# Six slots for the decode rows, six PSUM places for the memory's products, a later input load and one moved product

## What is computed

```python
def mem_kv(mem, g_mem, w_xkv):                       # 256 memory rows, 16 products of 128 features
    kk, vv = jnp.split(rmsnorm(mem, g_mem) @ w_xkv, 2, axis=-1)
    return kk.reshape(B, M, 4, 256), vv.reshape(B, M, 4, 256)

def cross_attn(xn, mk, mv, w_xq, w_xo):
    q = (xn @ w_xq).reshape(B, T, 4, 256)
    s = jnp.einsum('bthd,bmhd->bhtm', q, mk) * 256 ** -0.5
    p = jax.nn.softmax(s, axis=-1)
    return jnp.einsum('bhtm,bmhd->bthd', p, mv).reshape(B, T, 1024) @ w_xo

h = h + hybrid_mixer(rmsnorm(h, g_mix), ...)         # short conv and mLSTM heads
h = h + cross_attn(rmsnorm(h, g_cross), mk, mv, w_xq, w_xo)
h = h + swiglu(rmsnorm(h, g_ffn), w_gu, w_down)
```

## Time and profile before

| | us |
|---|---|
| median of 3 runs | 2920.24 (2918.0 to 2922.61) |
| the profiled execution | 2920.7 |
| its span, first to last instruction | 2918.9 |
| PE busy | 2865.0 (98%) |
| DVE busy | 1179.5 (40%) |
| ACT busy | 753.7 (26%) |
| POOL busy | 428.6 (15%) |
| mean granted TensorE clock | 0.993 |

### The profile page before, as it was taken

One profiled execution on the slowest core, in us unless ns is written; L12 is line 12 of the kernel. 1 busy time (PEld: TensorE's weight loads), 2 busy tenths in 40 slices (PEclk: granted clock), 3 DMA queues, 4 the chain that ended last, 5 costly groups with the idle time before them and its releaser, 6 DMA issues.

```text
span 2918.9 us, 38362 instructions
## 1 busy us (share of the span) xinstructions
PE 2865.0 (98%) x15739; PEld 2699.9 (92%) x15739; DVE 1179.5 (40%) x2258; ACT 753.7 (26%) x1467; POOL 428.6 (15%) x284
## 2 busy tenths in 40 slices
PE   7899999999999999999999999999999999999998
PEld 7788878888899999999998999998999999999998
DVE  6535645322533444234334547433422243342223
ACT  5543343232332220113222110322211022221001
POOL 1644434444310000001000101000000000000000
PEclk9999999999999999999999999999999999999999
DMA  6887778788686788768677889966667777667675
GB/s 238 297 353 277 285 241 307 287 291 311 233 316 213 265 303 297 272 239 328 224 287 282 317 321 398 352 243 251 230 232 258 260 261 283 221 245 254 250 271 184
DMA packets 144997, 801.14 MB, mean 274 GB/s; under 512 B 15948, under 2 KB 31692, under 8 KB 65080
## 3 DMA queue, kind: packets, MB, share of 16 engines
q1 hardware_dynamic: 119216, 719.10, 67.1%
q0 software_dynamic: 16208, 67.87, 6.6%
q10 hardware_dynamic: 9400, 11.72, 1.2%
HBM read 650.30 MB, written 148.33 MB: 274 GB/s over the span
## 4 chain that ended last, share of the span: by engine, by line
PE 93%; DMA 4%; DVE 1%; ACT 1%; issue 1%; POOL 0%; SPq 0%; ACTq 0%; DVEq 0%; POOLq 0%
PE gb L620 82%; PE gb L863 3%; PE ta L863 2%; PE td L863 1%; DMA w_raw<-w_kv 1%; DMA big<-kd_d 1%; DMA w_hl<-split_d 1%; DMA big<-x_blk 1%; PE ta L729 0%; DMA made_d<-big 0%; PE gb L667 0%; DMA w_raw<-w_dec 0%; DMA big<-rows_d 0%; PE gb L685 0%; PE gm L845 0%
## 5 line engine op out<-in xcount | busy, mean ns | idle before, releaser
L620 PE MATMUL gb<-xn_hi,w_hl 128*128 128x384 f32 (+2 forms) x5800 | 1582.8, 349 | 6.7 <-DVE big L1422 3.5
L620 PEld LDWEIGHTS gb<-xn_hi,w_hl 128*128 128x128 f32 x5800 | 1061.3, 188 | 55.3 <-issue 7.6
L620 PE MATMUL gb<-xn_lo,w_hl 128*128 128x384 f32 (+2 forms) x2920 | 1012.1, 347 | 0.0
L620 PE MATMUL gb<-act_hi,w_hl 128*128 128x384 f32 (+3 forms) x3296 | 869.9, 344 | 18.4 <-DVE w_hl L1390 11.3
L620 PEld LDWEIGHTS gb<-act_hi,w_hl 128*128 128x128 f32 x3296 | 599.8, 190 | 49.0 <-DVE w_hl L1390 11.6
L620 PEld LDWEIGHTS gb<-xn_lo,w_hl 128*128 128x128 f32 x2920 | 549.1, 188 | 24.3 <-issue 0.5
L620 PE MATMUL gb<-act_lo,w_hl 128*128 128x384 f32 (+3 forms) x1648 | 564.4, 342 | 0.0
L494 POOL TENSOR_TENSOR w_hl<-w_raw,w_hl 128x1024 fp32r<-128x1024 f32 x136 | 333.6, 2461 | 440.9 <-ACT w_hl L1007 440.8
L1441 DVE TENSOR_TENSOR work<-gb,r_res 128x384 f32<-128x384 f32 (+2 forms) x220 | 128.3, 586 | 583.1 <-PE gb L620 550.1
L620 PEld LDWEIGHTS gb<-act_lo,w_hl 128*128 128x128 f32 x1648 | 312.5, 190 | 12.3 <-issue 0.2
L1632 DVE TENSOR_TENSOR x<-x,gb 128x384 f32<-128x384 f32 (+2 forms) x200 | 115.5, 582 | 408.2 <-PE gb L620 404.7
(11 more groups left out here) (304 smaller groups left out, 2074.3 us busy)
## 6 DMA issues: line engine op xcount, KB each, us to landing
w_hl<-split_d SPq DMA_DIRECT2D x484, 1024.0 KB, 5.1
split_d<-w_hl SPq DMA_DIRECT2D x121, 1024.0 KB, 5.1
w_raw<-w_st SPq DMA_DIRECT2D x105, 512.0 KB, 6.6
w_raw<-w_kv SPq DMA_DIRECT2D x32, 512.0 KB, 4.3
made_d<-big ACTq DMA_DIRECT2D x32, 256.0 KB, 4.2
w_raw<-made_d SPq DMA_DIRECT2D x16, 512.0 KB, 8.2
big<-kd_d POOLq DMA_DIRECT2D x8, 1024.0 KB, 13.6
big<-vd_d POOLq DMA_DIRECT2D x8, 1024.0 KB, 12.9
```

The source lines that it names most:

```text
L620: mm = pe.matmul(gb[:, ps, 0:wd], a[:, s, k * P:(k + 1) * P], r[:, k, 0:wd], start=(first and k == ks[0] and i == 0), stop=(last and k == ...
```

## The change

Four things are changed.

1. `dwt` is all six slots of `w_raw`. Row i goes to slot i % 6 and waits for row i - 6; rows 4 and 5 of each eight are issued with the first four, and only rows 6 and 7 after the first group of four is used.
2. The memory's products g = 0 to 15 rotate through six places in PSUM: the three banks of `gb`, both of `ta`, and `gm` (`kv_bank`). PE waits ahead of product g until product g - 6 has been read, and not at all for g under 6. The pre-products wait for 12 + (16 + i) % 3, which are the products then in `gb`.
3. The first block's input is loaded by ACT's queue behind the three small decode loads, at the head of its g loop. DVE's wait for it goes; ACT's wait and the eight squares move from g = 0 to 3 to g = 7 to 10; `sumsq` and the norm move from g = 6 to g = 13.
4. In block 0 `xo(1, 1)` is issued ahead of `ptrans(2, 0)` and `ptrans(2, 1)`, not behind them.

```diff
-        dwt = w_raw[:, 2:6, :]
+        dwt = w_raw
...
+        def kv_bank(g):
+            return gb[:, g % 6, :] if g % 6 < NP else (ta[:, 0, :], ta[:, 1, :], gm[:, :])[g % 6 - NP]
...
             def decode_rows(i):
-                after(pool, dw_used, i - 3)
-                pool.dma_start(dwt[:, i % 4, :], w_dec[i] if i < KT else w_kv[G_MEM + i]).then_inc(dw_loaded[i % 4], 16)
+                after(pool, dw_used, i - NR + 1)
+                pool.dma_start(dwt[:, i % NR, :], w_dec[i] if i < KT else w_kv[G_MEM + i]).then_inc(dw_loaded[i % NR], 16)
...
-                    elif g >= NP:
+                    elif g < G_MEM:
+                        if g >= 6:
+                            read_out(pe, g - 6)
+                    else:
                         read_out(pe, g - NP)
+                bank = kv_bank(g) if g < G_MEM else gb[:, ps, :]
...
-                if g == 6:
+                if g == 13:
                     pe.wait_ge(mix_acc, 18)
...
-                    read_out(pe, G_MEM - NP + i)
+                    read_out(pe, 12 + (G_MEM + i) % NP)
...
                 xo(0, 1)
+                if b == 0:
+                    xo(1, 1)
                 ptrans(2, 0)
                 ptrans(2, 1)
-                xo(1, 1)
+                if b:
+                    xo(1, 1)
...
-                if k == 3:
-                    act.dma_start(x_next[:, :, 0:w0], x_blk[0:KT, :, 0:w0].rearrange("k p c -> p k c")).then_inc(x0_loaded, 16)
...
-            act.wait_ge(x0_loaded, 16)
             for g in range(G_MEM):
-                if g < 4:
-                    next_sq(0, 2 * g)
+                if g == 0:
+                    act.dma_start(x_next[:, :, 0:w0], x_blk[0:KT, :, 0:w0].rearrange("k p c -> p k c")).then_inc(x0_loaded, 16)
+                if 7 <= g < 11:
+                    if g == 7:
+                        act.wait_ge(x0_loaded, 16)
+                    next_sq(0, 2 * (g - 7))
                 w_high(g)
-                if g < 4:
-                    next_sq(0, 2 * g + 1)
-                if g == 6:
+                if 7 <= g < 11:
+                    next_sq(0, 2 * (g - 7) + 1)
+                if g == 13:
                     rnorm(r_mix, td, 2, w0, sq_mix)
...
-            v.wait_ge(x0_loaded, 16)
             for g in range(G_MEM):
```

More of the change, by code:

```diff
@@ L339, in trunk @@
         piece_done, do_ready, dox_t = sems("piece_done do_ready dox_t")
-        dw_loaded = sems("dw_loaded_0 dw_loaded_1 dw_loaded_2 dw_loaded_3")
+        dw_loaded = sems("dw_loaded_0 dw_loaded_1 dw_loaded_2 dw_loaded_3 dw_loaded_4 dw_loaded_5")
         cache_loaded = sems("cache_loaded_0 cache_loaded_1")
@@ L579, in _ @@
                     decode_caches()
-                    for i in range(4):
+                    for i in range(NR):
                         decode_rows(KT + i)
                 if b == DX:
-                    for i in range(4, KT):
+                    for i in range(NR, KT):
                         decode_rows(KT + i)
@@ L619, in gemm @@
                     for i, (a, r) in enumerate(passes):
-                        mm = pe.matmul(gb[:, ps, 0:wd], a[:, s, k * P:(k + 1) * P], r[:, k, 0:wd],
+                        mm = pe.matmul(bank[:, 0:wd], a[:, s, k * P:(k + 1) * P], r[:, k, 0:wd],
                                        start=(first and k == ks[0] and i == 0), stop=(last and k == ks[-1] and i == len(passes) - 1))
@@ L793, in decode_outputs @@
                     for i in range(t0, t0 + 4):
-                        pe.wait_ge(dw_loaded[i % 4], 16 * ((KT + i) // 4) + 16)
+                        pe.wait_ge(dw_loaded[(KT + i) % NR], 16 * ((KT + i) // NR) + 16)
                     for half, bank in enumerate((ta[:, 1, :], td)):
@@ L797, in decode_outputs @@
                             mm = pe.matmul(bank[32 * (i % 4):32 * (i % 4) + NDEC, :], dy[:, i * NDEC:(i + 1) * NDEC],
-                                           dwt[:, i % 4, half * 512:half * 512 + 512], start=i < 4, stop=i >= 4)
+                                           dwt[:, (KT + i) % NR, half * 512:half * 512 + 512], start=i < 4, stop=i >= 4)
                     mm.then_inc(dw_used, 4)
@@ L893, in decode_queries @@
                     for i in range(t0, t0 + 4):
-                        pe.wait_ge(dw_loaded[i % 4], 16 * (i // 4) + 16)
+                        pe.wait_ge(dw_loaded[i % NR], 16 * (i // NR) + 16)
                     for half, bank in enumerate((ta[:, 1, :], td)):
@@ L897, in decode_queries @@
                             mm = pe.matmul(bank[32 * (i % 4):32 * (i % 4) + NDEC, :], dxq[:, i, :],
-                                           dwt[:, i % 4, half * 512:half * 512 + 512], start=i < 4, stop=i >= 4)
+                                           dwt[:, i % NR, half * 512:half * 512 + 512], start=i < 4, stop=i >= 4)
                     mm.then_inc(dw_used, 4)
@@ L1405, in _ @@
                 v.wait_ge(group_done, g + 1)
-                v.tensor_tensor(dst[:, g % KT, :], gb[:, g % NP, 0:NMEM], r_res[:, 0:NMEM], ALU.mult).then_inc(out_v, 1)
-                if g < 4:
-                    next_sq(0, 2 * g)
+                v.tensor_tensor(dst[:, g % KT, :], kv_bank(g)[:, 0:NMEM], r_res[:, 0:NMEM], ALU.mult).then_inc(out_v, 1)
+                if 7 <= g < 11:
+                    next_sq(0, 2 * (g - 7))
                 if g + NS < G_MEM:
                     w_low(g + NS)
-                if g < 4:
-                    next_sq(0, 2 * g + 1)
+                if 7 <= g < 11:
+                    next_sq(0, 2 * (g - 7) + 1)
                 if g >= KT:
```

## The result

| | before | after |
|---|---|---|
| median of 4 runs | 2920.28 us (2918.0 to 2922.61) | 2901.88 us (2900.31 to 2903.2) |
| the profiled execution, its span | 2920.7, 2918.9 us | 2901.21, 2899.4 us |

The ratio is 0.9935 with a 95% interval of 0.992 to 0.995, 18.4 us by the medians. In the code after, lines stand 4 to 13 further down (L620 is L628, L1406 is L1418, L1710 is L1722, L1422 is L1434).

The account below looks back on a forecast made before the run. PE was taken as the bound, busy 2865.0 of 2918.9 us. Terms 7.8 - 1.5 + 2.6 + 4.4 + 6.1 - 0.5 = 18.9 us off 2920.7 gave 2901.8, forecast as 2901.5 us, range 2896.5 to 2910.

Parts of the forecast that it names:

- The stall and the clock behind it: Memory products, first block: PE's 5.2 us wait and 2.6 us of slow clock behind it both go, 7.8 us.
- The input there by 30 us: First block's input: issued at about 25 us, 2 MB at 415 GB/s would take 5 us; wanted at about 38.
- The give-back, 1.5 us: Pre-products: DVE, counted 3 us late from the squares, gives back 1.5 us of the gain; bounds 0 and 4.
- The sign I had named: Pre-products: the first one's wait was to grow by 1 to 2 us.
- My 8.9 for the two: First block with block 0's transposes: the predicted gains of 6.3 us and 2.6 us taken together.
- xo(1, 1): Block 0's transposes: wait falls from 3.2 to 1.9 us and the clock behind recovers, 2.6 us; bounds 1.4 and 3.0.
- Block 2's decode group: Wait of 2.8 us for decode rows goes and the slow group with it, 1.6 us; 4.4 us in all.
- Block 3's: Decode group in block 3: wait of 4.4 us goes, with some 1.7 for the slow group; 6.1 us.
- The extra megabyte: Split weights near 1806 us: costs 0.5 us, bounds 0 and 2.5; rival of full cost, 2905 us, 12%.
- the sums: Weights' stage, eight sums after product 13: rival that DVE falls further behind and PE stalls, 2904 us, 20%.
- the decode groups: Blocks 2 and 3: rival that rows 6 and 7 land late and the stalls stay, up to 2912 us, 6%.
- the late input: PE's wait ahead of `sumsq` behind product 13: rival that input landing after 40 us stalls PE, 2926 us, 2%.

Follow-up runs that it names:

- input_at_six: The changed kernel with the first block's input loaded six weights later on ACT, ahead of weight 12's split; median 2911.09 us, ratio to before 0.9963.
- after_again: The changed kernel run once more, unchanged, for a second trace; median 2899.11 us, ratio to before 0.9928.
- five_slots: The changed kernel with five slots for decode rows in place of six; median 2905.74 us, ratio to before 0.9943.
- three_places: The changed kernel with the memory's products back in three PSUM places, late input load and squares kept; median 2899.4 us, ratio to before 0.993.
- input_later: The changed kernel with the input's load moved to ACT's step g == 3, issued 1.1 us later; ratio to before 0.9934.
- slots_only: The kernel before with only the six decode slots added; median 2910.64 us, ratio to before 0.996.
- xo_only: The kernel before with only xo(1, 1) moved ahead of block 0's transposes; median 2919.72 us, ratio to before 0.9992.

## Why the prediction was right, and where not

The time was within 0.4 us of the median, and part of that is luck. By its steps:

**The stall and the clock behind it, 7.8 us.** Right: 8.1 us at the stage's end, of which 0.3 were there at the end of product 2 (25.36 against 25.7) and belong to no part of the change; PE at clock 1.00 without a gap, against 0.50 from 30 to 35 us before. Its reason is right as well. The experiments say which part of the edit matters: the late load alone does it all, and the places alone leave 2.2 us, for the squares beside the splits.

**The input there by 30 us.** Wrong and without effect. I took 2 MB at 415 GB/s, because in before the engines were nearly idle from 30 to 35 us (a share of 0.14). In after they are full from 30 to 40 us (1.01) and move 399 GB/s, 4 MB in 10 us, of which the input is at most 2. PE goes on there, so weight slots come free early and SP fills them: that is how I read the rest, and no run tests it. The DMA issue and the stretch, after:

```profile
DMA to landing us min/median/max: 13.4/13.4/13.4
```

```profile
30.00:40.00 10.00, 10.00 (x86) 10.00 (x85) 6.73 (x10) 3.85 (x5) 0.00 (x0) 1.00 1.01 399
```

It landed at 37.8, where ACT squared the first part at 37.95: no margin, where I had counted 8 us.

**The give-back, 1.5 us.** DVE's lag was there: the last sum at 54.4 (I had 55 to 56), PE ready at 56.9 by the timeline. PE began the long chain of pre-products at 79.72 and not at 86.95, so 8.1 us had become 7.2: 0.9 given back in place of 1.5. The sign I had named, a first wait grown by 1 to 2 us, didn't come: ahead of that chain it is 3.55 us in both, and a new one of 0.54 stands at 70.18. The last sum took 2.50 us in after and those before it 0.68 to 0.70, with POOL's splits running from 51.45 on, the first of them to 53.87; the sum, begun at 51.92, ended at 54.42. In input_at_six it was 2.43 us again, from 60.89, with POOL's splits from 60.42 on. PE's waits ahead of block 0 sum to 10.6 us, and to 11.5 before, so the 0.9 had come back by then: at the rows the lead was 9.1. What this pair of traces did lose, 3.0 us and 1.6 of low clock, it lost at the gates' rows, where I had no term. The 3.0 is the difference of the rows' transfers, 20.7 against 17.7 us, and by the other traces those are no longer with the lead than without it. A bound for it should have stood in the range all the same: from 120 to 180 us in the trace of before the DMA engines' share is 1.01 to 1.04 in each 10 us. How large it is changes: by the start of the same pair of `sumsq` matmuls at block 0's end, 462.2 us before, the first block with the transposes is worth 7.5, 9.3, 10.6 and 10.7 us in after, after_again, five_slots and three_places, 4.1 in input_later, and -2.4 in slots_only, which changes nothing there. My 8.9 for the two lies among them; that it is no further off is partly luck.

**xo(1, 1).** 2.9 us for 2.6; the wait is 1.9 as said, and the clock is 1.00 behind it (409.93 to 425 us in after). The bound of 3.0 was the better value.

**Block 2's decode group.** 4.5 for 4.4. From the first group on the piece list has nothing but matmuls at full rate (from 1558.73 to 1600 us in after, at clock 1.00).

**Block 3's.** 8.2 for 6.1: 4.4 of wait, 1.8 in the group and 0.4 in the product behind it (6.83 against 6.44), which I had as 1.7 together, and 1.6 in 36 matmuls at 2049.95 (9.91 against 8.29), which I missed. Nothing ties that last to the change: the same 36 took 9.89 us in slots_only and 9.73 in after_again, without a wait ahead of them, and 8.29 in xo_only, which had 5.9 us of wait. Six of the fourteen traces have the slow form, two of the three with four slots and four of the ten with six.

**The extra megabyte.** 0.8 us in this trace. But from 1713.8 to 1863.2 us, the time between the same two marks is 149.4, 149.9 and 149.5 us in the three traces with four slots and 148.6 to 150.8 in the ten with six, 149.6 in the mean of either. I took 0.5, with a bound of 2.5 that is my estimate, 1 MB at the 415 GB/s of the earlier trace rows. No run shows either as a term: by these times the megabyte costs nothing that can be told, and the transfer of split weights that PE waited for there took 21.55 us in before, 22.32 in after and 21.41 in slots_only.

No rival came: the sums were in time, the decode groups didn't wait, and the late input had to be forced. The luck in the total is that the 1.7 us too much in the first block and the 2.1 too little in block 3 fell in one pair of traces; both are of the size by which executions of one kernel differ.

## What to carry to other kernels

A stall in one trace is one draw: where its end was a transfer through full DMA engines (a share of 1.01 to 1.02), the same work gave 1.2 to 5.2 us, so read such a wait in several executions before it becomes a term, and give a fix a margin wider than the spread. A lead won at the start of a kernel has to be followed through the next stretch in which the DMA engines are full, where one execution may lose of it what another keeps (at block 0's end 7.5 us were left in after and 9.3 in after_again). And bytes that nobody waits for belong outside such a stretch: moved ahead of it or behind it, they took the wait at the gates' rows, 4.2 and 1.8 us in the two traces of the changed kernel, away in three kernels of three.

## What was not expected of the hardware

The granted clock fell in places with no wait just ahead: 36 matmuls behind 22 small ones took 8.29 us in eight traces and 9.7 to 9.9 in six, with identical work there. Over the 36 it was 1.00 in after and 0.85 in after_again, where it fell to 0.53 from 2030 to 2032 us and was 1.00 again from 2032 on. Nothing run here tells what decides it.
